# Query-weight preparation moved from the mixer's output stage into the cross-attention block

## What is computed

```
x = x + mix @ w_out                                  # output product of the mixer
h = rmsnorm(x, g_xattn[i])                           # "tokens"
m = rmsnorm(mem, g_mem[i])                           # "memory", 256 rows
q = rmsnorm((h @ wq).reshape(.., 4, 128), gq)        # query weights
k, v = split(m @ wkv, 2)                             # key weights, value weights
k = rmsnorm(k.reshape(.., 4, 128), gk)
p = softmax(q k^T / sqrt(128));  x = x + (p v) @ wo  # output weights
x = x + mlp(rmsnorm(x, g_mlp[i]))
```

## Time and profile before

| | us |
|---|---|
| three timed runs | 3102.57, 3099.40, 3103.34 |
| median | 3102.57 |
| profiled execution, its own time | 3102.57 |
| its span in the profile | 3100.8 |

### The profile page before, as it was taken

How to read it: one execution, slowest core, us unless ns; L and a number is a source line. 1 busy time by engine, 2 the same in 40 slices (tenths; PEclk the granted TensorE clock), 3 DMA queues, 4 the chain that set the end, 5 groups by cost and what they waited for, 6 DMA issues and landing times. The chain is left out here.

```text
span 3100.8 us, 36680 instructions
## 1 busy us (share of the span) xinstructions
PE 2814.6 (91%) x13802; PEld 2044.2 (66%) x13803; DVE 1620.0 (52%) x2423; ACT 1053.1 (34%) x1468; POOL 154.8 (5%) x171
## 2 busy tenths in 40 slices
PE   7877989999999899999966878999999999899982
PEld 6655768888878688888754665654766565466541
DVE  4864554444555544446855546652855454266413
ACT  4444443232224432233332241330634233144301
POOL 0530000000000000000012020000000000000002
PEclk9988999999999999999987788999999999999986
DMA  3110315444323132222210037999999899999994
GB/s 131 58 51 28 109 61 189 175 166 170 118 103 116 62 116 82 108 88 78 95 55 1 1 123 274 387 409 408 388 361 372 338 409 369 409 374 347 409 385 152
DMA packets 186386, 626.00 MB, mean 202 GB/s; under 512 B 9747, under 2 KB 15538, under 8 KB 185810
## 3 DMA queue, kind: packets, MB, share of 16 engines
q1 hardware_dynamic: 173328, 577.51, 49.1%
q10 hardware_dynamic: 10530, 37.02, 3.0%
q0 software_dynamic: 2304, 8.39, 0.7%
HBM read 581.73 MB, written 41.16 MB: 201 GB/s over the span
## 5 line engine op out<-in xcount | busy, mean ns | idle before, releaser
L91 DVE TENSOR_TENSOR unit_low<-unit_whole,unit_high 128x4096 fp32r<-128x4096 f32 (+3 forms) x95 | 287.3, 3029 | 177.4 <-ACT unit_high L88 165.5
L667 PE MATMUL psum<-tokens_high,unit_high 128*128 128x512 f32 (+2 forms) x1016 | 372.1, 366 | 4.4 <-PEq L873 1.6
L667 PE MATMUL psum<-tokens_high,unit_low 128*128 128x512 f32 (+2 forms) x1016 | 368.3, 363 | 0.0
L667 PE MATMUL psum<-tokens_low,unit_high 128*128 128x512 f32 (+2 forms) x1016 | 368.3, 362 | 0.0
L88 ACT ACTIVATE unit_high<-unit_whole 128x4096 fp32r<-128x4096 f32 (+2 forms) x65 | 225.8, 3474 | 377.1 <-PE psum L667 286.5
L88 ACT ACTIVATE moe_w_high<-ring_slot 128x1024 fp32r<-128x1024 f32 x208 | 215.9, 1056 | 60.0 <-PE psum L3804 59.1
L3627 PE MATMUL psum<-ring_slot,hT 128*64 128x512 f32 x1008 | 226.8, 599 | 7.5 <-DMA ring_slot<-in_moe_w_gu 7.5
L667 PEld LDWEIGHTS psum<-tokens_high,unit_high 128*128 128x128 f32 (+1 forms) x1016 | 190.9, 188 | 38.0 <-DVE unit_low L91 4.0
L667 PEld LDWEIGHTS psum<-tokens_low,unit_high 128*128 128x128 f32 (+1 forms) x1016 | 190.9, 188 | 31.6 <-issue 1.6
L667 PEld LDWEIGHTS psum<-tokens_high,unit_low 128*128 128x128 f32 (+1 forms) x1016 | 190.9, 188 | 30.6 <-issue 0.2
L667 PE MATMUL psum<-unit_high,hidden_high 128*128 128x512 f32 x512 | 199.5, 390 | 0.0
(11 more groups left out here) (642 smaller groups left out, 5351.8 us busy)
## 6 DMA issues: line engine op xcount, KB each, us to landing
ring_slot<-in_moe_w_gu SPq DMA_DIRECT2D x102, 2048.0 KB, 16.0
unit_whole<-in_moe_w_gu SPq DMA_DIRECT2D x34, 2048.0 KB, 12.9
ring_slot<-in_moe_w_down SPq DMA_DIRECT2D x34, 2048.0 KB, 12.3
ring_last_slot<-in_moe_w_down SPq DMA_DIRECT2D x34, 2048.0 KB, 15.7
unit_whole<-in_w_up SPq DMA_DIRECT2D x16, 2048.0 KB, 8.4
unit_whole<-in_w_down SPq DMA_DIRECT2D x16, 2048.0 KB, 7.6
expert_rows<-zero_row ACTq DMA_DIRECT2D x15, 1536.0 KB, 5.3
unit_whole<-in_w_in SPq DMA_DIRECT2D x5, 2048.0 KB, 7.7
```

The source lines that it names most:

```text
L91: return dve.tensor_tensor(self.low, self.whole, self.high.bitcast(F32), ALU.subtract)
L667: ins = pe.matmul(bank, a, c, start=(first and m == 0), stop=(last and m == len(parts) - 1))
```

## The change

Work on the key, query and value units is put at other places of the two blocks; nothing is added or left out:

- The mixer's block loads only the query weights (`u + 3`, the same unit as `keys + 1`); the load of the value weights moves into the cross block, whose SyncE list now has three loads.
- ScalarE's rounding of the query unit moves from just ahead of its last tile in the mixer's block to the head of its list in the cross block.
- VectorE's subtraction of the query unit moves from four quarters at the end of the mixer's block to one instruction at the head of its list in the cross block.
- The four quarters of the key unit, until now two ahead of the fifth bank's addition and two behind it, are subtracted one behind each addition of the fifth to eighth bank.

```diff
@@ mixer_out_and_norm, sync
                 sp.dma_start(gain[:, :], k.ins["g_xattn"][i].partition_broadcast(P)).then_inc(k.bias_loaded.sem, 16)
-                k.load_unit(sp, keys + 1)
-                k.load_unit(sp, keys + 2)
+                k.load_unit(sp, u + 3)
@@ mixer_out_and_norm, scalar
                         norm.round(act, FIRST + t - 1)
-                k.round_unit(act, keys + 1)
                 norm.round(act, FIRST + TT - 1)
@@ mixer_out_and_norm, vector
-                    if n == TT:
-                        k.rest_of_quarter(dve, keys, 0)
-                        k.rest_of_quarter(dve, keys, 1)
                     dve.wait_ge(k.bank_full.sem, k.bank_full.at(n + 1))
                     x = k.x[:, t, half * 512:half * 512 + 512]
                     dve.tensor_tensor(x, k.bank(n)[:, 0:width], x, ALU.add).then_inc(k.bank_free.sem, 1)
                     if half == 1:
+                        k.rest_of_quarter(dve, keys, t)
                         if t == 0:
-                            k.rest_of_quarter(dve, keys, 2)
                             dve.wait_ge(k.bias_loaded.sem, k.bias_loaded.at(16))
                         norm.scale(dve, FIRST + t)
-                        if t == 0:
-                            k.rest_of_quarter(dve, keys, 3)
-                        else:
+                        if t >= 1:
                             norm.rest(dve, FIRST + t - 1)
-                k.rest_of_quarter(dve, keys + 1, 0)
                 norm.rest(dve, FIRST + TT - 1)
-                for q in range(1, 4):
-                    k.rest_of_quarter(dve, keys + 1, q)
@@ CrossAttention.on_scalar
         k, MT = self.k, self.MT
+        k.round_unit(act, u + 1)
         for t in range(MT):
@@ CrossAttention.on_vector
         k, MT = self.k, self.MT
+        k.rest_of_unit(dve, u + 1)
         for t in range(MT):
@@ cross, sync
-                for j in range(1, 3):
+                for j in range(3):
                     k.load_unit(sp, u + j + 2)
```

## The result

| kernel | median us | lowest to highest | ratio to before, 95% interval |
|---|---|---|---|
| before | 3103.06 | 3099.40 to 3111.02 (6 runs) | |
| changed | 3122.83 | 3120.21 to 3125.15 (6 runs) | 1.0057 [1.0041, 1.0073] |

The change costs 19.8 us by the medians and 13 to 23 us by the interval. The profiled execution of the changed kernel took 3127.31 us with a span of 3125.6, 24.8 us over the span before.

What follows compares the result with a forecast made beforehand. TensorE was taken as the chain at the handover from mixer to cross attention. Per layer 9.38 us of delay plus 2.4 us of lost clock make 11.8, two layers 23.6: 3102.57 + 23.6 = 3126.2 us, range 3118.5 to 3131.

Steps and rivals of the forecast that it cites:

- The keys' remainder: Ahead of the first key bank: quarter 3 delays TensorE by 1.25 us, quarters 0 to 2 cost nothing.
- The load of the query weights: Issued at 366.1 instead of 352.21, it lands by 375.2, ahead of first use at 378.9, and costs nothing.
- The preparation: Head of the cross block: rounding 3.63 us, then subtraction 4.43 us, delay the first query product by 9.38 us, quarter included.
- the boundary: Between mixer's and cross block: its end holds every engine and takes 0.84 us before ScalarE may round.
- The clock: First query products: after 9.0 us idle TensorE runs at half clock, losing 2.4 us per layer, ends 1.6 and 2.7.
- such a dip of some 1.7 us: Elsewhere in a shifted stage: each layer can gain or lose a half-clock dip, 3122.8 to 3129.6 in all.
- What is moved behind it: Behind the query preparation: key copies, value and output weights come later but in time for use, costing nothing.
- The open boundary: Rival at the block's end: ScalarE is not held and rounds from 375.2; 8.0 us per layer, 3118.6; chance 0.04.
- a late load of the query weights: Ahead of the first query product: if slower than 12.8 us, the load would cost its excess; no chance given.
- a late load of the value weights: Rival: slowed by 8 us or more, it makes value products wait; each us beyond adds 2 us; chance 0.04.
- the absorption by the expert stage: Rival: expert weights' loads have their own date and swallow the delay; time stays at 3102.6; chance 0.04, other no-loss causes included.
- The kept clock: Rival at the query products: the clock holds, so a layer costs 9.38 us, time 3121.3; chance 0.08.

Runs made afterwards that it cites:

- the quarters put back: Changed kernel with the key unit's four quarters back where they were, so the query weights' load goes out earlier: 3127.67 us, run again 3123.54 us.
- the block experiment: Changed kernel with the query unit rounded and subtracted at the end of the mixer's block instead of the head of the cross block: 3112.16 us, 1.0026.
- the wait filled: Changed kernel with 32 filler products of 128x512 at the head of TensorE's list in the cross block: 3139.96 us.
- the spread alone: Kernel before with only the key unit's quarters spread, the query unit still prepared in the mixer's block: 3124.01 us, 1.0057.

## Why the prediction was right, point by point

- *The forecast.* 3126.2 us with 3118.5 to 3131 was set against 3122.83. The two profiled spans differ by 24.8 us where the sum said 23.6; the medians differ by 19.8. That the spans come so close to the sum is in part luck: the two seams, which are all that the sum is about, gave 21.9, and 2.9 came from stages with no edit. Both terms that made up the sum were somewhat too large.
- *The keys' remainder, +1.25 us.* The start of the key bank moved from 0.80 to 2.07 us behind the transposes: 1.27. The idle time in the row is 1.04 us and not 1.2 to 1.3, since the transposes end 0.23 us behind the start of the key bank in the kernel before (364.01 + 1.03 against 364.81). Quarters 0 to 2 cost nothing: TensorE has no wait there.
- *The load of the query weights, nothing.* Shown by the quarters put back: 13 us earlier, same wait of 8.57 us.
- *The preparation, +9.38 us with the quarter.* 9.04 and 9.05 us measured. The term that was too large is the boundary: I carried over 0.84 us, and it was 0.4. The two durations, 3.62 and 4.42 us, and the boundary that holds ScalarE were as told. The trace of the kernel before had the right value at other ends of blocks, as here:

```profile
484.01 0.36 PE L667 MATMUL psum<-tokens_high,unit_high 128*128 128x256 f32 x1 [0.41 <-PEq L980]
```

- *The clock, +2.4 us.* 7 and 11 slow steps in the changed kernel, 7 and 10 in the second execution. At 0.43 - 0.23 us each, with 0.3 for the first step, that is some 1.5 to 2.3 us: the right mechanism, but both under the 2.4 that I took, and the first layer just under the lower bound of 1.6. What follows the queries moves too: in the first layer the changed kernel lost another 1 us in a longer dip in the heads, and in the second it won 1 us, since the dip in the scores that the kernel before has is not there. The prediction named such a dip of some 1.7 us that comes or goes, and it is what happened. The Trainium skill, in "TensorE: Matmul & The Clock Gate", Part 1, says that the number of slow products varies from run to run of one kernel. The traces agree, if weakly: behind the same 8.57 us of idle time there are 7 slow steps in both executions of the first layer, and 11 and 10 in the second.
- *What is moved behind it, nothing.* The value unit was rounded from 395.25 and the output unit from 413.18, just behind the fourth query copy as worked out (413.5); no wait of TensorE on either.
- *The rivals.* The open boundary is refuted by the block experiment, a late load of the query weights by the quarters put back, and a late load of the value weights by its rounding, which starts 7.6 us after the issue (387.62 to 395.25), with the same waits of TensorE behind the queries as before. Against the absorption by the expert stage stands the changed kernel itself: it is 23.1 us late at the second layer's output products (1070.57 against 1047.45) and 24.8 us late at its end. With the first layer alone the profiled span is only 6.5 us longer, but its expert stage was also 3.4 us shorter than in the kernel before, which is within what that stage varies by, and the median is 11.7 us higher. The kept clock appeared only with the wait filled down to 0.64 us, and in one of two layers with 2.81 us left.
- *What I missed.* I costed the change as a whole and did not see that the spread alone would cost nearly as much in the old order (6.9 us a layer up to the query). Nor did I allow enough for the spread of the executions.

## What to carry to other kernels

Work that is hidden at the end of one block and moved to the head of the next loses its cover: it then costs the full length of each instruction in the chain, rounding plus subtraction, and the clock that TensorE loses meanwhile. When a split is delayed, look at what waits for it in the queues, since a load behind it can hold up an in-order engine that has other work. If preparation must stand on the path, do it in parts and let the consumer wait for each part. For effects of a few us in a kernel of 3 ms, compare the seam in the traces and not the totals, and count in it how long the clock was down, since that alone moved a seam by 1.7 us here in a stage with no edit.

## What the runs showed of the hardware that I had not expected

- The end of a block costs TensorE or VectorE about 0.4 us (0.39 and 0.41 in the rows shown) when its last work is a computation, and 0.78 to 0.91 us when SyncE issues a load at its very end, as at 376.79 before and 385.38 with the spread alone. The issue itself takes 0.37 us. I did not test it by itself.
- The clock fell after 2.45 us of idle time in one layer at once and in the other three steps later, after 2.81 us in one of two, and not after 0.64 us. It also fell with no idle time at all, behind 32 products of a single column (3.62 us), in both layers of the kernel before and not in the second layer of the changed one.
- An idle time of TensorE that the profile puts down to nothing ("issue"), at the same entry of a program, was 3.3 us in some kernels and 8.0 in others that differ only in code far ahead of it, which cost 13 us of 3,100. Its cause stays open.
